# Two SwiGLU layers on unnormed x: the reciprocal rms moved behind the product, the squares summed ahead of one ones-matmul

## The reference

```python
def rmsnorm(x, g):
    xf = x.astype(jnp.float32)
    inv = lax.rsqrt(jnp.mean(xf * xf, axis=-1, keepdims=True) + RMS_EPS)
    return (xf * inv).astype(x.dtype) * g

def swiglu_ffn(h, w_gate, w_up, w_down):
    return (jax.nn.silu(h @ w_gate) * (h @ w_up)) @ w_down

        h = rmsnorm(x, norm_ffn_g[layer])
        x = x + swiglu_ffn(h, ffn_w_gate[layer], ffn_w_up[layer], ffn_w_down[layer])
```

## Time and profile before

| | |
|---|---|
| device time, three runs | 3118.96, 3123.67, 3137.89 |
| median | 3123.67 |
| span of the profiled execution, first to last instruction | 3130.2 |
| the profiled execution's own device time | not shown apart; it is at least its span |
| PE busy | 2810.8 (90%) |
| POOL busy | 1689.3 (54%) |
| DVE busy | 1414.3 (45%) |
| ACT busy | 695.1 (22%) |
| mean granted TensorE clock | 0.958 |
| from one step to the next (first row of hidden to the next), without a wait for DVE | 38.0 (452.60 to 490.60) |
| the same, with one | 39.7 (530.29 to 570.02) |
| layer 0, entry's first instruction to its last add | about 230 to 680 |
| layer 1, the same | about 739 to 1195 |

### The profile page before, as it was taken

The page is one execution under the profiler, slowest core; times in us unless marked ns, Lnnn a source line. Parts: engine busy times, 40 slices in busy tenths (PEclk is TensorE's granted clock), DMA queues, the critical chain, the costliest instruction groups (busy, mean ns, idle before and its releaser), DMA issues.

```text
span 3130.2 us, 39049 instructions
## 1 busy us (share of the span) xinstructions
PE 2810.8 (90%) x13722; PEld 2242.6 (72%) x13722; DVE 1414.3 (45%) x1901; ACT 695.1 (22%) x1285; POOL 1689.3 (54%) x1014
## 2 busy tenths in 40 slices
PE   7588999986999997898997999999878888899997
PEld 5357887765787776755586888888666667678885
DVE  6954222248222227344416434433675555354444
ACT  2121000012000003355503001000254555110102
POOL 6237998875998885122435444444262121376661
PEclk9799999998999998999998999999989999999999
DMA  4013443431444342100011111111110010122221
GB/s 172 27 54 128 136 142 130 129 113 64 140 135 134 134 134 75 54 1 0 0 54 34 61 60 60 60 60 60 34 41 27 29 38 27 54 81 95 94 97 50
DMA packets 66449, 236.36 MB, mean 76 GB/s; under 512 B 7112, under 2 KB 8520, under 8 KB 66120
## 3 DMA queue, kind: packets, MB, share of 16 engines
q1 hardware_dynamic: 65800, 233.64, 22.7%
q10 hardware_dynamic: 576, 1.70, 0.2%
HBM read 233.22 MB, written 2.10 MB: 75 GB/s over the span
## 4 chain that ended last, share of the span: by engine, by line
PE 76%; DVE 11%; issue 6%; ACT 3%; POOL 2%; DMA 1%; DVEq 1%; ACTq 0%; POOLq 0%; SPq 0%
PE ps L411 59%; PE ps L690 3%; PE ps L542 2%; PE ps L445 2%; PE ps L792 2%; PE ps L764 1%; PE ps L676 1%; PE ps L814 1%; PE ps L460 1%; DVE rstd L1233 1%; POOL X L385 1%; DVE arena L1324 1%; PE ps L661 1%; DVE tmp L1238 1%; PE ps L653 1%
## 5 line engine op out<-in xcount | busy, mean ns | idle before, releaser
L353 POOL TENSOR_TENSOR wlo<-raw,whi 128x1024 fp32r<-128x1024 f32 x430 | 1058.4, 2461 | 35.9
L351 POOL TENSOR_SCALAR whi<-raw 128x1024 fp32r<-128x1024 f32 x430 | 486.8, 1132 | 1068.7 <-DMA raw<-in_stream 1067.0
L411 PE MATMUL ps<-Ahi,whi 128*128 128x512 f32 (+1 forms) x2208 | 765.0, 377 | 140.3 <-DVE Alo L1260 40.0
L411 PE MATMUL ps<-Alo,whi 128*128 128x512 f32 (+1 forms) x2208 | 759.4, 374 | 0.0
L411 PE MATMUL ps<-Ahi,wlo 128*128 128x512 f32 (+1 forms) x2208 | 758.7, 374 | 0.0
L411 PEld LDWEIGHTS ps<-Ahi,whi 128*128 128x128 f32 x2208 | 396.4, 193 | 229.4 <-issue 49.0
L411 PEld LDWEIGHTS ps<-Ahi,wlo 128*128 128x128 f32 x2208 | 395.7, 192 | 73.7
L411 PEld LDWEIGHTS ps<-Alo,whi 128*128 128x128 f32 x2208 | 396.3, 193 | 70.8
L411 PE MATMUL ps<-hhi,whi 128*128 128x512 f32 x1120 | 378.1, 375 | 37.8 <-DVE X L1618 21.3
L411 PE MATMUL ps<-hhi,wlo 128*128 128x512 f32 x1120 | 370.7, 368 | 0.0
L411 PE MATMUL ps<-hlo,whi 128*128 128x512 f32 x1120 | 370.5, 368 | 0.0
(11 more groups left out here) (196 smaller groups left out, 3199.6 us busy)
## 6 DMA issues: line engine op xcount, KB each, us to landing
raw<-in_stream SPq DMA_DIRECT2D x430, 512.0 KB, 3.7
X<-in_xT SPq DMA_DIRECT2D x2, 1024.0 KB, 6.3
arena<-in_dft SPq DMA_DIRECT2D x1, 2048.0 KB, 16.6
out_xT<-X SPq DMA_DIRECT2D x2, 1024.0 KB, 4.3
X<-in_ctxT SPq DMA_DIRECT2D x1, 1024.0 KB, 18.3
arena<-in_icnt ACTq DMA_DIRECT2D x1, 1024.0 KB, 5.0
vec<-in_vec SPq DMA_DIRECT2D x1, 364.5 KB, 7.8
arena<-in_fmap SPq DMA_DIRECT2D x1, 256.0 KB
```

Source lines behind the costliest of these rows:

```text
L351: pool.tensor_scalar(whi[:, s, part], raw[:, s, part], 1.0, 1.0, ALU.mult, ALU.mult).then_inc(sem("w_hi"), 1)
L353: pool.tensor_tensor(wlo[:, s, part], raw[:, s, part], whi[:, s, part], ALU.subtract).then_inc(sem("w_split"), 1)
L411: mm = pe.matmul(dst[c], w[:, b % RING, off:off + P], rhs(k, part, c0, n), start=(k == 0 and w is whi and part == 0), stop=(k == kn - 1 an ...
```

## The change

In both SwiGLU layers:

- ACT rounds X[k]*g straight into `Ahi`, as soon as X[k] is final and (layer 0) the last output-projection block has read the old `Ahi[k]`. DVE makes `Alo = X*g - Ahi` (`split_lo_gained`). Neither waits for the norm.
- DVE adds the eight tiles of squares up in `std` (`add_squares`, seven adds), and PE does one `ones` matmul on the sum, issued behind k = 5 of the entry's products (`SUM_AT`). Square root and reciprocal follow.
- PE starts the entry's ada blocks straight behind the stage before, in banks 4 and 5.
- The gate product is multiplied by rstd into `tmp[2+j]` on DVE (`scaled_gate`), Silu runs on `tmp` in place, the up product is multiplied by rstd into `tmp[j]` (`scaled_up`), and `hidden` multiplies the two tiles.
- The loads of `icnt` and of the attention tables are issued by ACT ahead of the norm's instructions.

```diff
             def columns(name, blocks, cols, dsts, ready=None, sums=None, read=None):
...
+                    if sums and k == SUM_AT:
+                        sums()
...
-            def swiglu(f, name, ready):
+            def swiglu(f, name, norm, evac):
+                def sums():
+                    pe.wait_ge(*when(f"{norm}_acc", KT - 1))
+                    pe.wait_ge(*when(evac, 7))
+                    pe.matmul(ps[:, 6, :], ones[:, :], std[:, 0:T], start=True, stop=True).then_inc(sem(f"{norm}_sum"), 1)
...
-                        pe.wait_ge(*when(f"{name}_silu" if part == 0 else f"{name}_mul", 2 * i))
+                        pe.wait_ge(*when(f"{name}_gate" if part == 0 else f"{name}_lin", 2 * i))
...
+                pe.wait_ge(*when(evac, 6))
                 for e in range(2):
-                    ada(B0 + e, (B0 + e) % RING, e)
-                columns(f"{name}_up", [(B0 + 2, B0 + 2), (B0 + 3, B0 + 3)], X_ONLY, banks[0:4], ready)
+                    ada(B0 + e, (B0 + e) % RING, e, bank=4)
+                columns(f"{name}_up", [(B0 + 2, B0 + 2), (B0 + 3, B0 + 3)], X_ONLY, banks[0:4], f"{norm}_out", sums)
...
-            rms("n2")
...
+            def rms_of_sums(name, g, ready, free, between):
+                def square(k):
+                    if k >= 4:
+                        act.wait_ge(*when(f"{name}_acc", max(1, k - 4)))
+                    act.activation(tmp[:, k % 4, 0:T], X[:, k, 0:T], ACT.Square).then_inc(sem(f"{name}_sq"), 1)
+                for k in range(KT):
+                    act.wait_ge(*ready(k))
+                    if free:
+                        act.wait_ge(*free(k))
+                    copy(Ahi[:, k, 0:T], X[:, k, 0:T], v(g[0], g[1] + k)).then_inc(sem(f"{name}_hi"), 1)
+                    if k < 4:
+                        square(k)
+                between()
+                for k in range(4, KT):
+                    square(k)
+                act.wait_ge(*when(f"{name}_sum", 1))
+                act.activation(std[:, 0:T], ps[:, 6, :], ACT.Sqrt, scale=1.0 / D, bias=epsr[:, 0:1]).then_inc(sem(f"{name}_std"), 1)
...
-                        act.activation(tmp[:, 2 + j, 0:T], ps[:, j, :], ACT.Silu).then_inc(sem(f"{name}_silu"), 1)
+                        act.activation(tmp[:, 2 + j, 0:T], tmp[:, 2 + j, 0:T], ACT.Silu).then_inc(sem(f"{name}_silu"), 1)
...
+            def split_lo_gained(name, k, g):
+                dve.scalar_tensor_tensor(out=Alo[:, k, 0:T], in0=X[:, k, 0:T], scalar=v(g[0], g[1] + k), in1=Ahi[:, k, 0:T],
+                                         op0=ALU.mult, op1=ALU.subtract).then_inc(sem(f"{name}_out"), 1)
...
+                def scaled_gate(i, b_g, j):
...
+                    dve.tensor_tensor(tmp[:, 2 + j, 0:T], ps[:, j, :], rstd[:, 0:T], ALU.mult).then_inc(sem(f"{name}_gate"), 1)
...
-                    dve.tensor_tensor(tmp[:, j, 0:T], ps[:, 2 + j, :], tmp[:, 2 + j, 0:T], ALU.mult).then_inc(sem(f"{name}_mul"), 1)
+                    dve.tensor_tensor(tmp[:, j, 0:T], ps[:, 2 + j, :], rstd[:, 0:T], ALU.mult).then_inc(sem(f"{name}_lin"), 1)
+
+                def hidden(i, j):
+                    dve.wait_ge(*when(f"{name}_silu", 2 * i + j + 1))
+                    dve.wait_ge(*when(f"{name}_lin", 2 * i + j + 1))
+                    dve.tensor_tensor(tmp[:, j, 0:T], tmp[:, j, 0:T], tmp[:, 2 + j, 0:T], ALU.mult).then_inc(sem(f"{name}_mul"), 1)
```

More of the change, by code:

```diff
@@ L51 @@
 RMS_EPS = 1e-6
+SUM_AT = 5
 LN_EPS = 1e-5
@@ L129, in build @@
         share("sq", tiles)
-        share("sum", tiles)
+        share("sum", {n: 1 if n in ("n2", "n4") else KT for n in norms})
+        share("acc", {n: KT - 1 for n in ("n2", "n4")})
         share("std", {n: 2 if n in with_ctx else 1 for n in norms})
         share("rstd", {n: 1 for n in norms})
-        share("y", {n: KT for n in norms if n not in ("n3", "n5")})
+        share("y", {n: KT for n in norms if n not in ("n2", "n3", "n4", "n5")})
         for signal in ("hi", "out"):
@@ L142, in build @@
             pair = (kind + "0", kind + "1")
-            for signal in ("silu" if kind == "ff" else "relu", "mul", "hi", "h"):
+            for signal in ("silu" if kind == "ff" else "relu", "mul", "hi", "h", *(("gate", "lin") if kind == "ff" else ())):
                 for n, phase in enumerate(pair):
@@ L164, in when, with read_by @@
             return sem(name), count + shared.get(name, (name, 0))[1]
+        def read_by(k):
+            if k % 4 == 3:
+                return when("w_used", 2 * (B_WOUT + 3) + k // 4 + 1)
+            return when("wout_read", k + 1 - k // 4)
         def block_used(b):
@@ L419, in h_rhs, with columns @@
                 return lambda k, part, c0, n: (hhi, hlo)[part][:, slot, k, c0:c0 + n]
-            def columns(name, blocks, cols, dsts, ready=None):
+            def columns(name, blocks, cols, dsts, ready=None, sums=None, read=None):
                 for k in range(KT):
@@ L478, in dense @@
                         pe.wait_ge(*when(f"{name}_evac", 2 * i + 2 - slots))
-                    columns(f"{name}_done", blocks[i:i + 1 + both], cols, dst[2 * i:], ready if both else None)
+                    columns(f"{name}_done", blocks[i:i + 1 + both], cols, dst[2 * i:], ready if both else None,
+                            read=read if i == 3 else None)
             pe.wait_ge(*when("setup", 1))
@@ L532, in _, with ada @@
             pe.wait_ge(*when("cstd", 4))
-            dense("wout", B_WOUT, X_ONLY, "mix_out")
-            def ada(b, slot, e):
+            dense("wout", B_WOUT, X_ONLY, "mix_out", "wout_read")
+            def ada(b, slot, e, bank=6):
                 for k in range(KT):
@@ L991, in step @@
                         copy(hhi[:, slot, j, 0:T], tmp[:, j, 0:T]).then_inc(sem(f"{name}_hi"), 1)
+                rms_of_sums(*norm, lambda: rows(B0, 1, 4))
                 step(0, B0, 0, True)
@@ new lines, in add_squares @@
+            def add_squares(name):
+                for k in range(1, KT):
+                    dve.wait_ge(*when(f"{name}_sq", k + 1))
+                    if k == 1:
+                        dve.tensor_tensor(std[:, 0:T], tmp[:, 0, 0:T], tmp[:, 1, 0:T], ALU.add).then_inc(sem(f"{name}_acc"), 1)
+                        continue
+                    dve.wait_ge(*when(f"{name}_acc", k - 1))
+                    dve.tensor_tensor(std[:, 0:T], std[:, 0:T], tmp[:, k % 4, 0:T], ALU.add).then_inc(sem(f"{name}_acc"), 1)
@@ new lines, in _ @@
+            for j in range(10):
+                if j < 8:
+                    if j % 2:
+                        dve.wait_ge(*block_used(B_WOUT + j // 2))
+                    else:
+                        dve.wait_ge(*when("wout_done", j // 2 + 1))
+                    dve.tensor_tensor(X[:, j, 0:T], ps[:, j, :], X[:, j, 0:T], ALU.add).then_inc(sem("wout_evac"), 1)
+                if j == 5:
+                    for k in range(6):
+                        split_lo_gained("n2", k, ("ffn_g", 0))
+                if j >= 8:
+                    split_lo_gained("n2", j - 2, ("ffn_g", 0))
@@ L1365, in mods @@
                                       vec[:, bass.ds(8 * pair + a, 8)], ALU.add).then_inc(sem(f"{name}_ada"), 1)
-                def hidden(i, b_u, j, first=False):
+                def scaled_gate(i, b_g, j):
+                    if j:
+                        dve.wait_ge(*block_used(b_g))
+                    else:
+                        dve.wait_ge(*when(f"{name}_up", 2 * i + 1))
+                    dve.tensor_tensor(tmp[:, 2 + j, 0:T], ps[:, j, :], rstd[:, 0:T], ALU.mult).then_inc(sem(f"{name}_gate"), 1)
@@ L1392, in step @@
                     for j in range(2):
-                        hidden(i + 1, b + 3, j)
+                        scaled_gate(i + 1, b + 1, j)
+                    for j in range(2):
+                        scaled_up(i + 1, b + 3, j)
+                    for j in range(2):
+                        hidden(i + 1, j)
                     mods(i + 1)
@@ L1398, in step @@
                             hidden_lo(i + 1, slot, m)
+                add_squares(norm)
+                norm_rstd(norm, 1, T)
                 for j in range(2):
-                    hidden(0, B0 + 3, j, True)
-                mods(0)
+                    scaled_gate(0, B0 + 2, j)
+                for j in range(2):
+                    scaled_up(0, B0 + 3, j, True)
+                for j in range(2):
+                    hidden(0, j)
+                mods(0, 4)
                 for j in range(2):
```

79 lines of the change are left out of this document (36 added, 43 removed).

## The result

Time after: 3176.25, median of 4 runs (3172.3 to 3183.88), against 3122.42 for the kernel before in the same comparison (4 runs, 3118.96 to 3137.89). The two medians are 54 apart. The ratio on record is smaller than theirs, 1.0153 with an interval of 1.0128 to 1.0179, which is 40 to 56 of 3123.67, with 48 in the middle. The change makes the kernel slower. The forecast was 3157, slower by 33, with a range of 3126 to 3174: the right direction. By the median it is 19 too little and 2 past the top of its range; by the ratio, which gives 3171, it is 15 too little and inside the range. A second comparison, made with the last experiments, gave 3158.75 (7 runs, 3152.91 to 3177.22) and a ratio of 1.0114 (1.0079 to 1.0149), some 36 more, which is 3 from the forecast.

What follows compares the result with a forecast made beforehand. The prediction took PE to bound the kernel, waiting for weights at the entry and DVE in the steps. Entries -10, first steps +2, other steps +15.9 and +25.2 made +33, so 3123.67 became 3157; range 3126 to 3174.

Steps and rivals of the forecast that it cites:

- What bounds the kernel: Whole span: PE, busy 90%; entry weights only half a microsecond ahead of the norm; PE waits for DVE in 14 steps.
- The entry, -4.8 each: Entry of both layers: fewer ones-matmuls and an earlier ada start, then the weights decide; -4.8 per layer, -10 rounded.
- the window of 241.6 to 242.5: Layer 0's entry: when POOL's split has the up block's first half ready, 3.8 to 4.7 sooner than 246.33.
- First steps, +2: First step of each layer: PE's next ada waits behind two scaled ups and two hiddens on DVE; 1.0 each.
- Steps without a wait, 6 x 2.65 = 15.9: Six steps where PE had not waited: two-tile hiddens and lower parts delay the adds, PE 2.65 late in each.
- Its sign: In the trace after, PE waits before a down job in all 20 steps, 2.6 or more in total in each.
- Steps with a wait, 14 x 1.8 = 25.2: Fourteen steps where PE already waited for DVE: hiddens taking turns with POOL add 0.9 to 2.0, taken as 1.8.
- the term's top of 2.0: Steps with a wait: POOL's L353 gets in before hidden 0, and add 2 ends at 540.9, +2.0.
- the low-end rival: Steps with a wait: hidden 0 wins the seam between POOL's instructions every time, +0.9 each; 3144; chance 0.17.
- The turn-taking with POOL: End of each step: a two-SBUF-tile DVE instruction and a POOL split block each other; hidden rows of 1.5 to 2.
- The rival without a cost: Steps: the hiddens find POOL idle or slip in at its seams, costing nothing; -10 + 2 gives 3116; chance 0.08.
- in the terms of the median, 3123.67 + 33: Whole kernel: the sum of +33 on the profiled span of 3130.2 carried over to the median of runs, 3157.

Runs made afterwards that it cites:

- second pair of profiles: The kernel before and the changed kernel each profiled once more, nothing edited: 3123.69 and 3158.75.
- lo_late: The changed kernel with only the lower parts of hidden moved behind the eight adds of the step: 3135.78, ratio 1.0034 to the kernel before.
- steps_only: The kernel before with its own norm and entry but the change's ten steps, rstd set to 1: 3170.44, ratio 1.0141.

## Why the prediction was right or wrong, point by point

**What bounds the kernel.** Right: PE's waits for DVE in the steps and the chain of weights at the entry, there by POOL's split rather than by the load.

**The entry, -4.8 each.** Right: -5.7 and -3.5 in the first profiles (-7.0 and -4.1 in the second), -9.2 and -11.1 together for the sum's -10. The up block was ready at 241.9, in the window of 241.6 to 242.5 that the step gave. The ones-matmul stood at 259.2 for the text's 258, the squares were done at 250.9 for its 253 to 254.

**First steps, +2.** Smaller: 28.0 to 28.6 in layer 0 and 28.6 both times in layer 1, +0.6.

**Steps without a wait, 6 x 2.65 = 15.9.** Right: they grew by 2.5, 2.6, 2.6, 3.3, 2.6 and 3.4, 17.0 in all. Its sign, PE's waits of "2.6 or more in total in each", is met in 10 of the 20 steps of the changed kernel; the other ten have 2.02 to 2.56, and steps as those of 2.04 grew by 2.6 all the same.

**Steps with a wait, 14 x 1.8 = 25.2.** Twelve of them grew by 0.7 to 1.8, mean 1.5, 18.2 in all; the two others by 4.2 and 4.0, which lies beyond the term's top of 2.0. Those two ran for some 4 at TensorE's lower level, which no term had (below). Sum 26.4. That it comes out so near 25.2 is in part luck: at 1.5 each, 14 steps would have given 21. In the second pair of profiles both layers grew by 38.9 together, where the terms for the steps have 43.1. `lo_late` shows that the waits for add 0 and add 2 add up as worked out; the low-end rival, with 0.9 each, falls.

**The turn-taking with POOL,** on which all this rests, holds: L1440 has a mean of 1883 ns, in the 1.5 to 2 that was to show it. The rule of the Trainium skill ("SBUF — State Buffer", "Who interferes with whom") had been preferred to the count of instructions. The rows agree: 4.13 for two instructions beside POOL and 1.28 where POOL is silent. The rival without a cost, 3116, is out by `steps_only` at 1.0141.

**From the span to the median, which is the step that fell short.** The sum was +33, and the two layers with their entries gave +34.4 and, in the second pair of profiles, +27.8. Of the 19 missing between the medians of the first comparison, 12.2 arose past layer 1, in code that the change doesn't touch, with a lower granted clock there. Some 6 more came from the step "in the terms of the median, 3123.67 + 33": the profiled execution of before lay 8 above its median (span 3130.2, device time 1.8 more), that of after 2 above its own (3178.59 to 3176.25). The 1.4 of the layers makes up the rest. The step treated the difference of two medians of a few runs as if the clock were the same in both. The range gave it no term, though the runs of before spread over 19. The second comparison, with 36 by its ratio, lies 3 from the forecast, so a part of the 19 belongs to the first comparison's few runs.
